# Expert rows loaded before the third block, two ring places returned in halves, and a split last column block

## The reference, cut to what matters

```python
for i in range(2):                       # the first two blocks
    x = x + 0.5 * swiglu(rmsnorm(x), w_gate[i], w_up[i], w_down[i])
    x = x + attention(rmsnorm(x)) @ w_out[i]
    x = x + 0.5 * swiglu(rmsnorm(x), ...)
# the third block: attention, deepnorm and layer norm
x = layer_norm(ALPHA * x + moba_attention(x) @ a_w_out, g0, b0)
# the experts: gate_up is [32, 1024, 2048], down is [32, 1024, 1024]
logits = x @ w_router + b_router
top4 -> shares
y = sum over the chosen experts of share * (act(x @ w_gate_up[e] + b) @ w_down[e] + b)
out = layer_norm(ALPHA * x + y, g1, b1)
```

## Time and profile before

| what | us |
|---|---|
| median of 3 runs | 2054.86 (2053.01 to 2058.71) |
| the profiled execution, its own time | 2054.72 |
| its span, first to last instruction | 2052.8 |
| TensorE busy in the span | 1979.5 (96%) |
| VectorE busy | 896.8 (44%) |
| ScalarE busy | 687.7 (33%) |

### The profile page before, as it was taken

One profiled execution on the slowest core, in us unless ns is written; L12 is line 12 of the kernel. 1 busy time (PEld: TensorE's weight loads), 2 busy tenths in 40 slices (PEclk: granted clock), 3 DMA queues, 4 the chain that ended last, 5 costly groups with the idle time before them and its releaser, 6 DMA issues.

```text
span 2052.8 us, 29213 instructions
## 1 busy us (share of the span) xinstructions
PE 1979.5 (96%) x12315; PEld 1378.8 (67%) x12315; DVE 896.8 (44%) x1074; ACT 687.7 (33%) x946; POOL 53.3 (3%) x42
## 2 busy tenths in 40 slices
PE   8999999999999999999999999999999999999997
PEld 8999778999999887999998444444334333433343
DVE  5766665676666678666644311111111111111112
ACT  5545475445554557444444111011101010100012
POOL 0700000000000000000000002000000000000000
PEclk9999999999999999999999999999999999999999
DMA  8664707655555542555295999999999999999997
GB/s 298 219 208 150 236 1 240 211 184 184 185 185 189 199 152 78 187 199 189 90 335 242 419 427 428 427 428 428 428 428 429 429 428 428 428 429 428 428 427 316
DMA packets 165724, 602.86 MB, mean 294 GB/s; under 512 B 9346, under 2 KB 102486, under 8 KB 140336
## 3 DMA queue, kind: packets, MB, share of 16 engines
q1 hardware_dynamic: 165484, 601.76, 75.2%
q10 hardware_dynamic: 164, 0.04, 0.0%
HBM read 600.68 MB, written 1.09 MB: 293 GB/s over the span
## 4 chain that ended last, share of the span: by engine, by line
PE 69%; DMA 22%; DVE 4%; ACT 3%; issue 1%; SPq 0%; DVEq 0%; ACTq 0%
PE ps L1913 13%; PE ps L1911 13%; PE ps L1912 13%; PE ps L2526 12%; PE ps L2552 5%; DMA sb_raw<-in_moe_w_down 5%; DMA sb_raw<-in_moe_w_gate_up 3%; DMA sb_nat_more<-in_moe_w_gate_up 3%; DMA sb_w_free<-in_moe_w_gate_up 3%; DMA sb_late_raw<-in_moe_w_down 3%; DMA sb_w_free<-in_moe_w_down 3%; PE ps L2491 2%; ACT sb_w_hi L711 1%; PE ps L2502 1%; DVE sb_w_lo L1165 1%; PE ps L2560 1%
## 5 line engine op out<-in xcount | busy, mean ns | idle before, releaser
L1165 DVE TENSOR_TENSOR sb_w_lo<-sb_raw,sb_w_hi 128x2048 fp32r<-128x2048 f32 x175 | 403.0, 2311 | 229.1 <-ACT sb_w_hi L711 228.6
L711 ACT ACTIVATE sb_w_hi<-sb_raw 128x2048 fp32r<-128x2048 f32 x179 | 340.5, 1912 | 160.2 <-PE ps L1913 139.5
L1911 PE MATMUL ps<-sb_xT_hi,sb_w_hi 128*128 128x256 f32 x1344 | 372.4, 277 | 0.0
L1912 PE MATMUL ps<-sb_xT_lo,sb_w_hi 128*128 128x256 f32 x1344 | 371.8, 277 | 0.0
L1913 PE MATMUL ps<-sb_xT_hi,sb_w_lo 128*128 128x256 f32 x1344 | 371.7, 277 | 0.0
L1912 PEld LDWEIGHTS ps<-sb_xT_lo,sb_w_hi 128*128 128x128 f32 x1344 | 252.9, 188 | 1.5
L1911 PEld LDWEIGHTS ps<-sb_xT_hi,sb_w_hi 128*128 128x128 f32 x1344 | 252.3, 188 | 1.7 <-DVE sb_w_lo L1165 0.2
L1913 PEld LDWEIGHTS ps<-sb_xT_hi,sb_w_lo 128*128 128x128 f32 x1344 | 252.3, 188 | 0.0
L1785 DVE COPY sb_h_rows<-ps 128x512 f32<-128x512 f32 x31 | 21.4, 692 | 315.0 <-PE ps L2526 315.0
L1077 ACT ACTIVATE sb_h_rows<-ps 128x512 f32<-128x512 f32 x32 | 19.2, 599 | 413.4 <-PE ps L2526 413.4
L1913 PE MATMUL ps<-sb_w_hi,sb_a_lo 128*128 128x512 f32 x352 | 138.7, 394 | 0.0
(11 more groups left out here) (333 smaller groups left out, 2693.2 us busy)
## 6 DMA issues: line engine op xcount, KB each, us to landing
sb_raw<-in_moe_w_gate_up SPq DMA_DIRECT2D x49, 2048.0 KB, 34.5
sb_w_free<-in_moe_w_gate_up SPq DMA_DIRECT2D x46, 2048.0 KB, 34.5
sb_raw<-in_ffn_w_up SPq DMA_DIRECT2D x44, 1024.0 KB, 5.3
sb_raw<-in_ffn_w_down SPq DMA_DIRECT2D x44, 1024.0 KB, 5.0
sb_raw<-in_moe_w_down SPq DMA_DIRECT2D x22, 2048.0 KB, 33.9
sb_raw<-in_ffn_w_gate SPq DMA_DIRECT2D x43, 1024.0 KB, 5.4
sb_w_free<-in_moe_w_down SPq DMA_DIRECT2D x21, 2048.0 KB, 33.9
sb_late_raw<-in_moe_w_gate_up SPq DMA_DIRECT2D x17, 2048.0 KB, 35.3
```

What stands on the lines that cost most here:

```text
L711: sc.activation(w_hi[:, c % CUT, :], raw[:, c % RAW, :], ACT.Copy).then_inc(hi_made, 1)
L1165: ve.tensor_tensor(w_lo[:, c % CUT, :], raw[:, c % RAW, :], w_hi[:, c % CUT, :].bitcast(F32), ALU.subtract).then_inc(lo_made, 1)
L1911: pe.matmul(o, l_hi, r_hi, start=start, stop=False)
L1912: pe.matmul(o, l_hi, r_lo, start=False, stop=False)
```

## The change

It has three parts. First, 1 MB of place 3 (row 0 of chunk 3 of expert 0) and 0.5 MB of `kept_more` (row 0 of a down chunk of expert 28) are loaded before the third block's weights, and the loads that were there bring only the rest. Second, PE raises `half_used` after the first 8 of the 16 matmuls on places 0 and 1 in `first_step`, and SP refills each of these places in two loads of 1 MB. Third, the last 512 columns of b = 1 in the third block's output projection are made as two runs of 256 columns in two PSUM banks, and VectorE adds, and takes statistics, in halves.

```diff
+            halves_more = 16 * (t % RING < 2 and (t >= RING or not isinstance(r, int)))
...
+            sp.wait_ge(turned, 4 * t_of(1, T_O) + 8)
+            sp.dma_start(nat_more[:, 0, :], gate_up_rows_of(0, 3)[:, 0, :]).then_inc(ahead_loaded, 16)
             sp.wait_ge(o_made, u_moba)
+            sp.dma_start(kept_more[:, 0, 0:D], down_rows_of(KEPT_E, 1)[:, 0, :]).then_inc(kept_loaded[1], 16)
...
             expert_chunk("gate_up", 0, 2, 2)
-            expert_chunk("gate_up", 0, 3, 3)
+            sp.dma_start(nat_more[:, 1, :], gate_up_rows_of(0, 3)[:, 1, :]).then_inc(slot_loaded[3], 16)
...
-            sp.dma_start(kept_more[:].rearrange("p a (k n) -> p (a k) n", k=2), whole_rows(1)).then_inc(kept_loaded[1], 16)
+            sp.dma_start(kept_more[:].rearrange("p a (k n) -> p (a k) n", k=2)[:, 1:4, :],
+                         whole_rows(1)[:, 1:4, :]).then_inc(kept_loaded[1], 16)
...
-            step_loads(0, 0, first=2)
+            for j in (2, 3):
+                dst, src = slots[j - 2].rearrange("p (a n) -> p a n", a=2), gate_up_rows_of(1, j)
+                sp.wait_ge(half_used, j - 1)
+                sp.dma_start(dst[:, 0, :], src[:, 0, :]).then_inc(slot_loaded[j - 2], 16)
+                sp.wait_ge(chunk_used, used_no(j - 2, 0))
+                sp.dma_start(dst[:, 1, :], src[:, 1, :]).then_inc(slot_loaded[j - 2], 16)
...
+                        if stats:
+                            for q in range(2):
+                                ve.wait_ge(*((out_half, outs_before + 2), (chunk_used, c + 2))[q])
+                                cols = x[:, 1, 512 * n + 256 * q:512 * n + 256 * (q + 1)]
+                                ve.scalar_tensor_tensor(out=cols, in0=cols, scalar=add, in1=ps[:, (bank + 1, 4)[q], 0:256],
+                                                        op0=ALU.mult, op1=ALU.add).then_inc((out_added, proj_read)[q], 1)
+                                ve.wait_ge(*((out_added, outs_before + 2), (proj_read, g + 1))[q])
+                                ve.bn_stats(row_stats[:, 1, 2 + q, :], cols).then_inc(stats_made, 1)
+                            stats(1)
...
+                        elif x_ahead is None and b == 1:
+                            ins = out_rows(g0, c0, 1, h, b, quarter=0)
+                            if h == 1:
+                                ins.then_inc(out_half, 1)
+                            ins = out_rows(g0, c0, 1, h, b, quarter=1)
...
+                    if half and k == 0:
+                        ins.then_inc(half_used, 1)
                 ins.then_inc(chunk_used, 1)
...
+                    if j == 3 and isinstance(r, int):
+                        pe.wait_ge(ahead_loaded, 16)
+                    gate_up_rows(left, j, j, 0, r, half=isinstance(r, int) and j < 2)
```

More of the change, by code:

```diff
@@ L161, in build @@
         turn_by = bt[:, 512:1024].rearrange("p (t b w d) -> p t b w d", t=2, b=TB, w=2)
-        row_stats = sb("row_stats", [P, TB, 2, 6])
+        row_stats = sb("row_stats", [P, TB, 4, 6])
         mean_var = sb("mean_var", [P, TB, 2])
@@ L310, in build @@
             sem("down_bias_added"))
+        ahead_loaded, half_used = sem("ahead_loaded"), sem("half_used")
         y_hi_made, y_lo_made, last_scattered, ln1_loaded, first_rows = (
@@ L339, in loaded_no @@
             n = t // RING + 1 - len([k for k in left_out if k < t]) + laps
-            return 16 * n + 16 * (ROUND_C // RING - len(left_out)) * r
+            halves_more = 16 * (t % RING < 2 and (t >= RING or not isinstance(r, int)))
+            return 16 * n + 16 * (ROUND_C // RING - len(left_out)) * r + halves_more
         g_kv, g_in, g_out = (lambda i: 8 * i), (lambda i: 8 * i + 1), (lambda i: 8 * i + 6)
@@ L485, in small_loads @@
                     sp.dma_start(pos_i[:], a["positions"][0].rearrange("(b p) -> p b", p=P)).then_inc(small_loaded, 16)
+            gate_up_rows_of = lambda e, j: a["moe_w_gate_up_2"][0][e, 256 * j:256 * (j + 1), :].rearrange("(p k) n -> p k n", k=2)
+            down_rows_of = lambda e, j: a["moe_w_down_2"][0][e, 512 * j:512 * (j + 1), :].rearrange("(p k) n -> p k n", k=4)
             for i in range(2):
@@ L1283, in project @@
                     if n == n_groups - 1:
-                        for b in range(TB):
+                        for b in range(1 if stats else TB):
                             if b and first_tile:
@@ L1301, in project @@
                         ve.wait_ge(proj_read, g + 1)
-                        for b in range(TB):
-                            ve.bn_stats(row_stats[:, b, n, :], x[:, b, 512 * n:512 * (n + 1)]).then_inc(stats_made, 1)
+                        ve.bn_stats(row_stats[:, 0, n, :], x[:, 0, 512 * n:512 * (n + 1)]).then_inc(stats_made, 1)
+                        for q in range(2):
+                            ve.bn_stats(row_stats[:, 1, q, :], x[:, 1, 256 * q:256 * (q + 1)]).then_inc(stats_made, 1)
             def heads(t, n):
@@ L1515, in spread @@
                 def spread(b):
-                    ve.wait_ge(stats_made, 3 + b)
-                    ve.bn_aggr(mean_var[:, b, :], row_stats[:, b].rearrange("p a b -> p (a b)")).then_inc(first_ln_step, 1)
+                    ve.wait_ge(stats_made, 4 + 2 * b)
+                    ve.bn_aggr(mean_var[:, b, :],
+                               row_stats[:, b, 0:2 + 2 * b].rearrange("p a b -> p (a b)")).then_inc(first_ln_step, 1)
                     ve.wait_ge(first_ln_step, b + 1)
@@ L1557, in last_layer_norm @@
                 ve.wait_ge(ln_step, 2)
-                ve.bn_aggr(mean_var[:, 0, :], row_stats[:, 0].rearrange("p a b -> p (a b)")).then_inc(ln_step, 1)
+                ve.bn_aggr(mean_var[:, 0, :], row_stats[:, 0, 0:2].rearrange("p a b -> p (a b)")).then_inc(ln_step, 1)
                 ve.wait_ge(ln_step, 3)
@@ L2046, in ffn_phase, with out_rows @@
                 ffn_out(c0 + FFN_C - 1, 0, g0 + FFN_PAIRS - 1, last=True, x_ahead=x_ahead)
-            def out_rows(g0, c0, n, h, b, ks=range(4)):
+            def out_rows(g0, c0, n, h, b, ks=range(4), quarter=None):
                 g, c = g0 + n, c0 + 2 * n + h
+                bank, cols = 2 * (g % 2) + b, slice(0, 512)
+                if quarter is not None:
+                    bank, cols = (bank, 4)[quarter], slice(0, 256)
                 pe.wait_ge(lo_made, c + 1)
@@ L2054, in out_rows @@
                     kk = 4 * h + k
-                    w = slice(k * 512, (k + 1) * 512)
+                    w = slice(k * 512, (k + 1) * 512) if quarter is None else slice(k * 512 + 256 * quarter,
+                                                                                    k * 512 + 256 * (quarter + 1))
                     l = slice(b * P, (b + 1) * P)
-                    ins = three(ps[:, 2 * (g % 2) + b, :], xT_hi[:, kk, l], xT_lo[:, kk, l], w_hi[:, s, w], w_lo[:, s, w],
+                    ins = three(ps[:, bank, cols], xT_hi[:, kk, l], xT_lo[:, kk, l], w_hi[:, s, w], w_lo[:, s, w],
                                 kk == 0, kk == KT - 1)
@@ L2512, in bias, with gate_up_rows @@
                               bias_parts[:, col + 512 * h:col + 512 * (h + 1)], start=True, stop=False)
-            def gate_up_rows(left, t, j, laps, r, in_halves=False):
+            def gate_up_rows(left, t, j, laps, r, in_halves=False, half=False):
                 if in_halves:
@@ L2535, in down_rows @@
                 if t in KEPT_T:
-                    pe.wait_ge(kept_loaded[j], (32, 16)[j])
+                    pe.wait_ge(kept_loaded[j], 32)
                 elif first_half is not None:
@@ L2591, in first_step @@
                     pe.wait_ge(xs_made, g + j + 1)
-                    gate_up_rows(left, j, j, 0, r)
+                    if j == 3 and isinstance(r, int):
+                        pe.wait_ge(ahead_loaded, 16)
+                    gate_up_rows(left, j, j, 0, r, half=isinstance(r, int) and j < 2)
                     if j < 2:
```

## The result

The changed kernel takes 2072.24 us (median of 4 runs, 2069.60 to 2073.12); the kernel before, run beside it, 2053.94. The ratio is 1.0083, with a 95% interval of 1.0071 to 1.0094. The change makes the kernel about 18 us slower, where 2.3 us of gain were forecast.

What follows compares the result with a forecast made beforehand. The second half was taken as bound by one DMA stream of expert rows plus a fixed tail. Room 2.5 us less 0.2 us PE delay gave 2.3 us gain: 2054.72 to 2052.4, as median 2052.5 us; range 2050.0 to 2056.0.

Steps and rivals of the forecast that it cites:

- 12 matmuls of 512 columns become 24 of 256 ... That is nothing: PE, last 512 columns of b = 1: both forms take 2.75 us, so halving costs PE nothing.
- something that I haven't seen: Catch-all case for an outcome outside the named ones, anywhere in the kernel; chance 0.04.
- What would make it wrong: Signs: last landing moves under 1 or over 3.7 us, expert 0's first matmul over 0.5, or PE waits before 1250.
- The room: Ring load issued at 1190.7: issue to landing 10.1 us minus the lone load's 7.6 lets the stream come 2.5 us earlier.
- the gaps named near 1140 and before 1200: Expert stream: DMA share below 1 for a microsecond or two at these times.
- the rival with 8.8 us as the floor: Smaller room at load 1190.7: 1.3 us, PE 0.37 us later, gain 0.9 us, 2054.0 us; chance 0.20.
- Worth 0 to 0.6 us of the sum: Refills of places 0 and 1 near 1140: the halves feed the emptying queue, already counted within the room.
- The rival that each load pays its lone cost: Expert stream: two more loads each cost 2.7 us extra, net 1.7 us slower, 2056.6 us; chance 0.03.
- the fixed cost: Expert stream: about 2 us per DMA by the skill's rule; two additional loads would take 4 us, sum 0.3 us slower.
- 0.37 forecast: VectorE, last 512 columns of b = 1: halves take 0.37 us more, making PE 0.2 us later.
- I cost this side at nothing: 1.5 MB loaded ahead of the third block costs nothing there, at most 4.6 us without the idle stretch.
- The clock: Rival: TensorE's clock falls before expert 0, PE loses 3.45 us, 2056.0 us; chance 0.04.

Runs made afterwards that it cites:

- e1: Kernel before with 96 unused bytes per partition behind mean_var, no instruction changed, distance 32 instead of 192: 2071.47 us, ratio 1.0089.
- e8: Changed kernel with qscale and stat moved ahead of the cut weights, keeping the old distance (xT_hi address minus w_hi, modulo 256): 2057.79 us, ratio 1.0013.
- e17: Changed kernel without the column halves, with the kept_more load issued ahead of the gains, biases and masks: 2053.67 us, ratio 1.0000.
- e15: Kernel before with the halves of places 0 and 1 alone, every address and other load as before: ratio 1.0003.
- the ten: Ten traces without early rows, of the kernel before and address kernels with raw anywhere but 96 bytes on: stream lengths 933.45 to 933.84 us.
- e19: Kernel before with the column halves alone, and qscale and stat moved ahead of the cut weights to keep the distance: ratio 1.0000.
- e10: Changed kernel without the column halves, so row_stats and every address stay as before: 2056.80 us, ratio 1.0009.
- e9: Kernel before with qscale and stat moved ahead of the cut weights, xT staying where it was, distance 96: 2088.83 us, ratio 1.0165.
- e20: Changed kernel with qscale and stat moved ahead of the cut weights, and the kept_more load issued ahead of gains, biases and masks: ratio 1.0005.

## Why the prediction was wrong

**The step that failed first is one that isn't there.** The prediction has no word on `row_stats`, which grows with the change, and the sum has no term for what stands behind it in SBUF: it stands at nothing without a reason. The step "12 matmuls of 512 columns become 24 of 256 ... That is nothing" rests on rows taken at distance 192; at distance 32 the 4608 matmuls of 256 columns and some 2000 of 512 got slower. Measured: 18.0 us (e1 alone, 2071.47 against 2053.44; the change with the old distance, e8, is within 0.03 to 0.23% of before). The case "something that I haven't seen" had a chance of 0.04 and held the outcome. "What would make it wrong" did work: the first matmul of expert 0, forecast at 1137.9, came at 1156.1.

**The room.** "From that load on the stream can come forward by 2.5 us" failed too. Taken for itself the change's stream is between 0.3 us longer (changed kernel and e1, the same addresses: 933.95 and 933.64) and 0.4 us shorter (e17), not 2.3 shorter. The mechanism was right in kind: PE's releases limit how early a load can come, and the gaps named near 1140 and before 1200 are there (0.86 and 0.87 in e17). Three things were wrong in size or missing. First, the 1 MB taken from the first burst let it run dry 14 us in, ahead of loads that wait for `o_made`; the prediction put no gap there. Second, the floor was the lone load's 7.6 us. The load in question fell from 10.1 only to 9.6 in the changed kernel and 8.6 in e17, where the engines had run dry: the room is 1.5 us and not 2.5, near the 1.3 of the rival with 8.8 us as the floor. Third, everything behind this load was taken as kept, and slips, set against those of the kernel before, took 1.1 of e17's 1.5 us. What brings the last of them isn't settled.

**The halves of places 0 and 1.** "Worth 0 to 0.6 us of the sum": e15 alone 1.0003 (0.9994 to 1.0013), stream length within the ten. Right, in that nothing can be measured. The rival that each load pays its lone cost has nothing for it: e15 adds two loads, and the stream isn't longer. The same goes for the fixed cost in the section "Anatomy of one DMA" of the Trainium skill ("DMA: Bandwidth & Descriptors"), on which the prediction draws: the section describes loads issued by GpSimd, and SyncE issues these.

**The column halves.** Mechanism and size right: VectorE 0.31 us longer (0.37 forecast), PE 0.11 us later at the first expert matmul (39.46 against e1's 39.35 behind the first issue; 0.2 forecast), and no time of their own (e19, 1.0000).

**The early loads' own side.** "I cost this side at nothing" held: from the third block's first chunk to the burst are 121.5 us before and 121.6 in e10.

**The clock.** The rival named the stretch ahead of expert 0, and there nothing fell. Where it did fall, behind the second attention, it took 3.4 us at most, and e1 has this fall as well.

## What to carry to other kernels

A tensor that grows moves all that is allocated behind it. Before a change is priced, list which operands of hot matmuls change their distance, and make up for it with a few bytes of padding, or put the new bytes at the end. When the loss shows ahead of the first changed instruction, compare the step of one repeated matmul in both traces, before reading anything of the changed code. A lead handed to a long full queue isn't a gain until the last landing shows it: it is lost where the engines run dry, and a landing waits for the slowest of the 16 engines.

## What the runs showed of the hardware that was not expected

- The pace of a matmul with 128 x 128 weights depends on where its two SBUF operands lie to each other, modulo 256 bytes per partition: medians of 113 to 120 ns for 256 columns and 226 to 237 ns for 512, at a granted clock of 1.00. The best distance differs by form: 192 for 256 columns (`w` loaded as weights, `xT` streamed), 0 for 512 (`xT` or `a` loaded as weights, `w` streamed, 227 ns). Width and roles change together here, so that the runs don't tell which of them matters, nor why distance does. The Trainium skill ("SBUF — State Buffer", section "Operand start alignment") asks only for a start at a multiple of the element's size and says that this is about legality, not speed. All kernels here keep to it, and their medians are up to 35.7 us apart.
- At one distance two paces can hold, 113 and 118 ns, each for tens of microseconds.
- In a full queue a load lands with the slowest of the 16 DMA engines. One packet of 16 KB from an instruction queue can put an engine 1.2 us behind the other 15, and it stays behind (e17, above); 36 of 37 late landings have such a packet just ahead of them.
- DMA writes depend on the place as well. With `raw`, `w_free` and `nat_more` 96 bytes further (e8, e9, e19, e20), a 2 MB load of the stream lands every 4.902 us instead of 4.894 (over 117 loads), in all four; with 32, 64 or 320 bytes it stays at 4.894 to 4.895. From 1500 to 1990 us, the kernel before and then e9:

```profile
DMA packets 14413, 209.90 MB, mean 428 GB/s; under 512 B 1602, under 2 KB 1602, under 8 KB 1602
```

```profile
DMA packets 14394, 209.64 MB, mean 428 GB/s; under 512 B 1599, under 2 KB 1599, under 8 KB 1599
```

  That is 0.12 to 0.16% of the rate, 1.2 to 1.5 us over the stream, and it is why e8, e19 and e20 have stream lengths of 934.6 to 935.5.
